# The triangular inverse in a chunked RWKV-7 recurrence: levels 1 to 4 on 32x32 tiles of TensorE, level 5 on other PSUM banks

## What is computed

```python
def _wkv_scan(s0, r, w, k, v, kk, a, reverse):
    def step(s, inp):
        r_t, w_t, k_t, v_t, kk_t, a_t = inp
        sa = jnp.einsum("bhvk,bhk->bhv", s, -kk_t)
        s = (s * w_t[:, :, None, :] + sa[..., None] * (kk_t * a_t)[:, :, None, :]
             + v_t[..., None] * k_t[:, :, None, :])
        return s, jnp.einsum("bhvk,bhk->bhv", s, r_t)
    xs = tuple(jnp.moveaxis(z, 1, 0) for z in (r, w, k, v, kk, a))
    s_fin, ys = lax.scan(step, s0, xs, reverse=reverse)
    return jnp.moveaxis(ys, 0, 1), s_fin
```

## Time and profile before

| | us |
|---|---|
| median of 3 runs | 2581.51 |
| lowest and highest | 2579.84, 2581.87 |
| the profiled execution | 2582.96 |
| its span, first to last instruction | 2581.1 |
| chunk stage of layer 0 | about 322 to 526 |
| chunk stage of layer 1 | about 1248 to 1452 |

### The profile page before, as it was taken

How to read it: one execution, slowest core, us unless ns; L and a number is a source line. 1 busy time by engine, 2 the same in 40 slices (tenths; PEclk the granted TensorE clock), 3 DMA queues, 4 the chain that set the end, 5 groups by cost and what they waited for, 6 DMA issues and landing times.

```text
span 2581.1 us, 47722 instructions
## 1 busy us (share of the span) xinstructions
PE 2403.9 (93%) x19861; PEld 1849.5 (72%) x19861; DVE 1623.0 (63%) x1820; ACT 1174.1 (45%) x1243; POOL 171.2 (7%) x260
## 2 busy tenths in 40 slices
PE   5999889987999999899789959999999999999998
PEld 2446389943888785556689748888888888888886
DVE  3474556444333333484455349898989898989897
ACT  3341422212222222443222137676767676767675
POOL 0000054300000000000444000000000000000000
PEclk9999999998999999999899979999999999999999
DMA  7221700052333225221000439898989898989897
GB/s 274 66 82 66 261 4 4 20 196 82 98 98 98 82 80 210 66 84 57 2 4 20 181 131 374 318 374 316 365 319 367 317 371 312 363 327 373 310 372 268
DMA packets 233285, 497.58 MB, mean 193 GB/s; under 512 B 9398, under 2 KB 78284, under 8 KB 226092
## 3 DMA queue, kind: packets, MB, share of 16 engines
q1 hardware_dynamic: 230960, 481.10, 51.6%
q10 hardware_dynamic: 2172, 14.20, 1.5%
HBM read 488.98 MB, written 6.29 MB: 192 GB/s over the span
## 4 chain that ended last, share of the span: by engine, by line
PE 86%; DVE 5%; ACT 3%; issue 3%; POOL 2%; DMA 1%; ACTq 0%; DVEq 0%; POOLq 0%
PE ps L551 17%; PE ps L553 17%; PE ps L552 17%; PE ps L628 11%; PE ps L825 10%; PE ps L544 7%; PE ps L579 2%; POOL tail L2158 2%; ACT weight_parts L1485 2%; PE ps L853 2%; PE ps L602 1%; PE ps L1101 1%; PE ps L984 1%; DVE tail L1931 1%; DVE tail L1885 1%
## 5 line engine op out<-in xcount | busy, mean ns | idle before, releaser
L2066 DVE TENSOR_TENSOR weight_parts<-front,weight_parts 128x2048 fp32r<-128x2048 f32 x336 | 767.8, 2289 | 85.2 <-ACT weight_parts L1485 84.6
L1485 ACT ACTIVATE weight_parts<-front 128x2048 fp32r<-128x2048 f32 x336 | 642.2, 1918 | 245.1 <-PE ps L553 245.0
L551 PE MATMUL ps<-weight_parts,token_parts 128*128 128x512 f32 x1344 | 533.8, 397 | 16.2 <-DVE token_parts L2073 16.2
L552 PE MATMUL ps<-weight_parts,token_parts 128*128 128x512 f32 x1344 | 526.3, 392 | 0.0
L553 PE MATMUL ps<-weight_parts,token_parts 128*128 128x512 f32 x1344 | 526.1, 391 | 0.0
L551 PEld LDWEIGHTS ps<-weight_parts,token_parts 128*128 128x128 f32 x1344 | 253.6, 189 | 71.8 <-DVE token_parts L2073 18.1
L1182 ACT ACTIVATE tail<-ps 128x512 f32<-128x512 f32 (+2 forms) x219 | 124.2, 569 | 393.8 <-DVE tail L1849 170.6
L628 PE MATMUL ps<-front,tail 128*128 128x512 f32 (+3 forms) x704 | 286.1, 563 | 12.4 <-ACT front L1256 7.6
L553 PEld LDWEIGHTS ps<-weight_parts,token_parts 128*128 128x128 f32 x1344 | 254.0, 189 | 54.8
L552 PEld LDWEIGHTS ps<-weight_parts,token_parts 128*128 128x128 f32 x1344 | 254.3, 189 | 51.0
L825 PE MATMUL ps<-tail 64*64 64x64 f32 x7808 | 258.1, 220 | 32.2 <-POOL tail L2158 15.4
(11 more groups left out here) (222 smaller groups left out, 2309.1 us busy)
## 6 DMA issues: line engine op xcount, KB each, us to landing
front<-in_exp_w SPq DMA_DIRECT2D x342, 1024.0 KB, 5.7
tail<-in_ffn_w SPq DMA_DIRECT2D x30, 1024.0 KB, 5.0
tail<-in_ada_w SPq DMA_DIRECT2D x27, 1024.0 KB, 8.7
tail<-in_w_in SPq DMA_DIRECT2D x24, 1024.0 KB, 5.1
front<-in_ada_w SPq DMA_DIRECT2D x21, 1024.0 KB, 8.9
tail<-in_w_out SPq DMA_DIRECT2D x8, 1024.0 KB, 5.1
parked_x<-front ACTq DMA_DIRECT2D x2, 2048.0 KB, 8.9
front<-parked_x ACTq DMA_DIRECT2D x2, 2048.0 KB, 9.3
```

The lines of the kernel that those rows point to most:

```text
L551: mm(view, a_hi, b_hi, start=start, stop=False)
L552: mm(view, a_lo, b_hi, start=False, stop=False)
L1485: f_(whi[k % PARTS], at(A_RING2 + (k % RING2) * SLOT2, SLOT2), ACT.Copy).then_inc(cnt["act"].sem, 1)
L2066: ins = v.tensor_tensor(wlo[m % PARTS], at(A_RING2 + (m % RING2) * SLOT2, SLOT2), whi[m % PARTS], ALU.subtract)
```

## The change

`blocks` takes the place of `small` for levels 1 to 4: for each of the 8 pairs of matrices (2 directions x 4 columns of heads) it issues four matmuls of 32x32 with 32 columns, one for each group q of 32 partitions, on the four diagonal 32x32 tiles of the array. That is 32 matmuls in place of 16. The halves off the diagonal blocks are no longer written. So that they read as zero, DVE clears banks 0 and 1 once per layer at the stage's start, after their last earlier reader (`uses_before`), and `level` waits for `cleared`. Level 5 stays 64x64 and whole, and its two products move from banks 0 and 1 to the turning banks 5, 6, 7.

```diff
--- before.py
+++ after.py
@@ -465,7 +465,7 @@
         n_small = sum(len(t) for t in VEC_TILES) + 1
         xload_v = 16 * 4
 
-        used_by = {}
+        used_by, uses_before = {}, {}
         norm_no = {(0, 0): 0, (0, 1): 1, (1, 0): 2, (1, 1): 3, (2, 0): 4}
         w_base = [0, 16]
         LG, MX, R1, R2, CHO, SC, RI, CI, R3, R4, R5 = 0, 8, 16, 24, 32, 40, 48, 59, 70, 78, 86
@@ -807,6 +807,7 @@
 
             def chunks(l):
                 banks.all_free(pe)
+                uses_before[l] = banks.uses[0:2]
                 pe.wait_ge(ev("rates_used"), 8 * (l + 1))
                 pe.wait_ge(ev("values_final"), CC * (l + 1))
 
@@ -826,6 +827,18 @@
                                          start=begin and d == 0 and cc == 0, stop=end, skip_group_check=True)
                     if end:
                         banks.fill(ins, key)
+
+                def blocks(key, a, b, bank):
+
+                    where = banks.take(pe, key, bank)
+                    for d in range(2):
+                        for cc in range(CC):
+                            for q in range(4):
+                                r, c = slice(32 * q, 32 * q + 32), slice(q % 2 * 32, q % 2 * 32 + 32)
+                                at_ = (d * CC + cc) * CH + q % 2 * 32
+                                ins = mm(where[r, at_:at_ + 32], a[r, d, cc, c], b[r, d, cc, c],
+                                         start=d == 0 and cc == 0, stop=True, skip_group_check=True)
+                    banks.fill(ins, key)
 
                 def of(tile):
                     return lambda d, cc, r: tile[r, d, cc, :]
@@ -869,14 +882,21 @@
 
                     pe.wait_ge(ev("mt_ready"), mt_no(l, n, b) + 1)
                     pe.wait_ge(ev("x_ready"), (LEVELS - 1) * (STEPS * l + n) + b)
-                    small(("T", l, n, b), of(MT[mt_no(l, n, b) % N_MT]), of(X), 0)
+                    if b < LEVELS - 1:
+                        pe.wait_ge(ev("cleared"), 2 * (l + 1))
+                        blocks(("T", l, n, b), MT[mt_no(l, n, b) % N_MT], X, 0)
+                    else:
+                        small(("T", l, n, b), of(MT[mt_no(l, n, b) % N_MT]), of(X), next(turn))
 
                 def doubled(b, n):
 
                     banks.released(pe, ("T", l, n, b))
                     if b > 1:
                         banks.released(pe, ("XT", l, n, b - 1))
-                    small(("XT", l, n, b), of(T1), of(XT[n % 2]), 1)
+                    if b < LEVELS - 1:
+                        blocks(("XT", l, n, b), T1, XT[n % 2], 1)
+                    else:
+                        small(("XT", l, n, b), of(T1), of(XT[n % 2]), next(turn))
 
                 turn = itertools.cycle((5, 6, 7))
                 for n in range(-2, STEPS):
@@ -1821,6 +1841,9 @@
                 t0 = first(l)
                 every = lambda t: t.rearrange("p a b c -> p (a b c)")
                 idb = idc.unsqueeze(1).broadcast_to([P, 2 * CC, CH])
+                for b, n in enumerate(uses_before[l]):
+                    dve.wait_ge(banks.free[b], n)
+                    v.memset(psum[b], 0.0).then_inc(ev("cleared"), 1)
                 for h in range(CC):
                     banks.released(dve, ("on", l, h))
```

## The result

The changed kernel takes 2663.11 us (median of 4 runs, 2657.10 to 2666.90) against 2581.69 us: a ratio of 1.0305, 95% interval 1.0288 to 1.0323. It is slower by 81 us where 29 us less were forecast, and outside the range. The profiled execution is the one of 2666.9 us, 84 us above that of before.

What follows compares the result with a forecast made beforehand. Layer 0's chunk stage was taken as bound by PE, while layer 1's first steps also wait. Savings of 10 x 1.5 + 4 x 2.0 + 6.6 = 29.6, taken as 29 us, gave 2552 us; range 2528 to 2592.

Steps and rivals of the forecast that it cites:

- The product: Levels 1 to 4: a block product on four tiles takes 0.53 us where a 64x64 one takes 0.93, saving 0.40.
- two tiles at a time: Rival: tiles overlap only in twos, a block product takes 1.01 us, the kernel 2613 us; chance 0.09.
- The switch: Change of tile shape around each block product: 0.12 us going in, 0.15 coming back, 0.27 per product.
- DVE, ACT and POOL; memsets, `cleared`, banks: 0: Other engines do not become the bound; clearing, its wait and level 5's bank move cost 0 us.
- 0.4 + 1.1 + 0.1 us a step: Switch costs per full step: between XT and next T 0.4, between T and XT 1.1, R product ahead of T1 0.1.
- what fills a round: Per-tile pass time: 0.84 ns per column plus 4.8 ns, so 31.6 ns a round for 32 columns on four tiles.
- 7 x 1.5 and half of 6.6: Savings: 1.5 us per full step, and 6.6 us for both layers' inversions ahead of step 0.
- Slower: Outcome class: the changed kernel comes out slower than before; chance 0.22.
- Instructions set the pace: Rival: each pass still costs 29 ns, a block product 1.87 us, 171 us over forecast, 2723 us; chance 0.08.
- the clock falls: Rival: smaller pieces lower TensorE's clock; a quarter of each stage at 1.2 GHz gives 2654 us; chance 0.03.
- 2.8 - 0.4 - 0.8: Saving per step in layer 0's four steps with the 3.31 us reciprocal, given as 1.5 us.
- between 9 and 13 ns: Rival: a 32x32 pass lands at 9 to 13 ns, the kernel at 2566 to 2592 us; chance 0.10.

Runs made afterwards that it cites:

- the kernel without blocks: The changed kernel with levels 1 to 4 whole as 64x64 products again, memsets, `cleared` and level 5's banks kept: 2589.91 us, ratio 1.0007 against the kernel before.
- the burst: 64x64 products throughout, plus repeated products that wait for nothing (32x32, 32-column and full 64x64 forms) ahead of each layer's first inversion: 2685.09 us, one run.
- the kernel with half of the blocks: The changed kernel with block products of direction 0 only, the second direction left out at levels 1 to 4: 2556.17 us, ratio 0.9870 against the kernel before.
- the 64x32 tiles: The changed kernel with each block product as the full 64x64 product in 32 matmuls on 64x32 tiles: 2663.74 us, ratio 1.0286 against the kernel before.

## Why the prediction was wrong

**The product: 0.53 us on four tiles, 0.40 saved.** Right to some hundredths of a us wherever nothing interrupts it: 7.9 ns a pass had been taken, and undisturbed products take 0.56 us from first start to last, 8.9 ns a pass. The rival of two tiles at a time falls with it. The rule of the Trainium skill (TensorE: Matmul & The Clock Gate, "Wait — 56ns, not 53.3ns?") that starts never come closer than about 25 ns is contradicted in its wording, since 64 starts lie in 0.56 us. Yet 3.67 us for 128 passes is 29 ns a pass over a long dense stretch. The sum needed that as a least time for every 128 passes. As a price of each product it gives the rival's 2723 us, which is too much.

**The switch: 0.12 in, 0.15 out.** Right in sum to some hundredths of a us. From the last pass of a block product to the next shape it is 0.12 us by start times (the 0.68 us from 412.11 are 0.56 and 0.12), and from a 64x64 pass into the next block product 0.15, where the pass alone would take 0.03.

**DVE, ACT and POOL; memsets, `cleared`, banks: 0.** Right within 0.2%: the kernel without blocks measures 1.0007, and the three engines' busy times in a step are those of before. Which switches lie on the path, 0.4 + 1.1 + 0.1 us a step, no run shows apart.

**The step that failed is "the product", where it took what fills a round as the only price of a pass, and so put the supply of instructions at nothing.** What the runs showed in its place is a least time for every 256 instructions, 128 passes: 3.67 us on average in the burst, and never under 3.3 in the changed kernel's steps. I let twice the instructions come in half the time and priced their supply nowhere in the sum. What I said on it stood under a rival ("twice the instructions in the same time were never asked of this queue"), and I answered it with eight loads that started within 0.05 us of each other. Eight are far fewer than the 256 of a page: a burst says nothing about supply. A row that could have told stood on the page of the profile as q8, 125 packets, and their distances in the stage, 4.16 us on average and never below 3.31, against 3.72 us that a page of 64x64 passes lasts.

What that term cost: the kernel with half of the blocks and the change differ by 31 packets and 107 us, 3.45 us each. In layer 0 the waits of TensorE by "issue" (349 to 560 us of the changed kernel) come to 35.4 us where the kernel before has 1.7 in its layer-0 steps:

```profile
PE ps L839 <- issue: 22.2, 25, 3.5
PE ps L826 <- issue: 10.8, 14, 1.4
PE ps L866 <- issue: 2.4, 3, 1.0
```

42 interruptions, each some 0.2 us longer by start times than by the modelled ends (427.54 to 427.97 is 0.43 us, the row has 0.22), so about 44 us, 42 more than before. The stage grew by 34.7, and the difference, some 8 us, is an estimate of what the shorter products still gave back; the sum had 7 x 1.5 and half of 6.6, some 14, for this layer.

**The rivals.** Slower was given 0.22. "Instructions set the pace" had the right side and the wrong form: an even 29 ns in every pass and 171 us, where it is an interruption per page, hidden where other work stretches the page; that is why 111 us and not 171 came on top of the forecast. Nearest in number was "the clock falls" (2654), by luck: it named another cause. A fall of the clock is there as well, as a consequence: in layer 0 the clock stays at 0.97, but in layer 1 it was 0.50 in the first inversion and about 0.85 in the early steps, behind the new gaps. Layer 1 lost about 9 us more than layer 0, and I count most of that for it. No run holds the clock with the gaps, so that share is argued and not shown. It is hardly all of the 9: with the 64x32 tiles the steps of layer 1 ran at 0.97 to 1.00, and its stage still grew 3 us more than layer 0's over the kernel without blocks (42.2 against 39.1, from the first pass to the last). Two slips of the working move nothing: 2.8 - 0.4 - 0.8 is 1.6 and not 1.5, and 2566 us, the lower end of "between 9 and 13 ns", belongs to 9.6 ns a pass.

## What to carry to other kernels

Count instructions as a resource of their own: for a stream of small matmuls, compare the time that 256 instructions (128 passes of fp32) take there with what a page needs (3.67 us in the burst here), or with the least distance between packets of the instruction queue in the same trace. If the stretch is near that, smaller tiles can't pay, however well they overlap. Idle time that is called "issue" and comes back after equal counts of instructions is the sign. The mean over a step isn't enough, since a slow page gives nothing to a fast one. And before an edit shrinks a matmul, a burst of that form with nothing to wait for measures it in one run, at supply and clock as they are.

## What was not expected of the hardware

- A page of 256 instructions for TensorE took 3.67 us on average in a burst (3.47 to 4.01), with idle DMA engines, at either clock level. Its packet started 1.0 to 1.3 us after the page before it was entered, and 2.3 to 2.7 us ahead of its first pass.
- On 64x64 tiles a pass with 32 moving columns takes what one with 64 takes: 29 ns at the full clock, 53 ns at half.
- On four 32x32 tiles passes start 8 to 9 ns apart at the full clock (64 in 0.56 us); in the bursts at half clock 128 need 1.7 us to their last start.
- A wait instruction whose semaphore has long been raised costs TensorE's stream 98 ns when 32 stand in a row; 158 of them fewer, spread over the products and made by VectorE, changed nothing.
- The granted clock fell to its lower level (0.57 from 1320 to 1349 us, 0.50 in its later part) in a stretch in which no data was waited for, but TensorE stood still for about 2 us of every 3.7.
